# High-part passes of two weight tiles first, chunk inputs ahead of the taps on TensorE, third modulations ahead of the layer norm, and late small inputs

## The reference, cut to what matters

```python
def ada_mod(c, w, b):                      # modulations from the condition c
    return jax.nn.silu(c) @ w + b

def trunk_layer(x, c, conv_buf, h0_re, h0_im, lp):
    sh1, sc1, g1, sh2, sc2, g2 = jnp.split(ada_mod(c, w_ada, b_ada), 6, axis=-1)
    h = modulate(rms_norm(x, norm1_g), sh1, sc1)
    z = h @ w_in                           # 1024 -> 512 (a), 512 (gate), 512 (u)
    hc = a * jax.nn.sigmoid(gate)
    hc, new_buf = causal_depthwise_conv(hc, conv_buf, conv_w, conv_b)   # width 31
    hc = jax.nn.silu(layer_norm(hc, conv_ln_g, conv_ln_b))
    hs, hT_re, hT_im = s5_mixer(u, h0_re, h0_im, ...)   # 32 groups x 64 complex states
    mix = jnp.concatenate([hc, hs], axis=-1) @ w_out
    x = x + g1[:, None, :] * mix
    h2 = modulate(rms_norm(x, norm2_g), sh2, sc2)
    x = x + g2[:, None, :] * peer_ffn(h2, peer_w_q, peer_keys, peer_u, peer_v)
    return x, new_buf, hT_re, hT_im
```

## Time and profile before

| what | value |
|---|---|
| runs shown, median of 3 | 1868.39 us (1866.77 to 1869.2) |
| profiled execution, its own time | 1861.53 us |
| its span, first to last instruction | 1859.7 us |
| mean granted TensorE clock, share of full | 0.983 |
| TensorE matmuls busy | 1758.6 us (95%) |
| VectorE busy | 1186.8 us (64%) |
| ScalarE busy | 681.9 us (37%) |
| GpSimd busy | 689.5 us (37%) |

### The profile page before, as it was taken

How to read it: one execution, slowest core, us unless ns; L and a number is a source line. 1 busy time by engine, 2 the same in 40 slices (tenths; PEclk the granted TensorE clock), 3 DMA queues, 4 the chain that set the end, 5 groups by cost and what they waited for, 6 DMA issues and landing times.

```text
span 1859.7 us, 33440 instructions
## 1 busy us (share of the span) xinstructions
PE 1758.6 (95%) x13287; PEld 1635.7 (88%) x13287; DVE 1186.8 (64%) x3089; ACT 681.9 (37%) x1212; POOL 689.5 (37%) x585
## 2 busy tenths in 40 slices
PE   5997868999999999999999999999999999999996
PEld 2884557889999999999999999988888888888895
DVE  8987953159995677777776760256666666666663
ACT  2313323233333444444444444333333333333333
POOL 1200013335446333333333334466555555555200
PEclk9999889999999999999999999999999999999998
DMA  8454322548888788888888788689988889888831
GB/s 300 119 122 159 131 100 80 181 152 241 239 242 234 211 245 253 260 248 248 256 238 256 250 255 245 230 288 361 340 321 317 319 311 338 327 315 316 303 126 47
DMA packets 305707, 442.72 MB, mean 238 GB/s; under 512 B 24752, under 2 KB 221536, under 8 KB 303504
## 3 DMA queue, kind: packets, MB, share of 16 engines
q1 hardware_dynamic: 280416, 366.35, 61.8%
q0 software_dynamic: 25136, 74.24, 11.3%
HBM read 377.37 MB, written 130.25 MB: 273 GB/s over the span
## 4 chain that ended last, share of the span: by engine, by line
PE 88%; DVE 7%; DMA 2%; ACT 2%; issue 1%; POOL 1%; DVEq 0%; SPq 0%; ACTq 0%; POOLq 0%
PE ps L1823 40%; PE ps L1851 28%; PE ps L1582 8%; PE ps L1812 5%; PE ps L1802 3%; DVE conv_out L1146 1%; PE ps L1553 1%; PE ps L1536 1%; PE ps L1638 1%; DVE rstd L1052 1%; DMA v_rows_ring<-v_rows,v_row_index 1%; DMA raw<-in_w_ada 1%; PE ps L1722 0%; PE ps L1771 0%; DVE wt L928 0%
## 5 line engine op out<-in xcount | busy, mean ns | idle before, releaser
L1823 PE MATMUL ps<-h,hl 128*128 128x256 f32 (+1 forms) x6144 | 823.7, 288 | 1.4 <-DVE sc L1312 1.4
L1823 PEld LDWEIGHTS ps<-h,hl 128*128 128x128 f32 x6144 | 761.7, 189 | 1.6 <-DVE sc L1312 1.6
L819 ACT ACTIVATE hl<-raw 128x512 fp32r<-128x512 f32 x512 | 322.4, 630 | 730.3 <-PE ps L1823 475.6
L1851 PEld LDWEIGHTS ps<-WH,hl 128*128 128x128 f32 x3072 | 531.7, 188 | 30.3 <-issue 28.5
L1851 PE MATMUL ps<-WH,hl 128*128 128x384 f32 x3072 | 545.1, 337 | 1.3 <-ACT actr L851 1.3
L618 POOL TENSOR_TENSOR hl<-raw,hl 128x512 fp32r<-128x512 f32 x260 | 352.2, 1356 | 500.5 <-ACT hl L819 500.5
L1492 DVE TENSOR_TENSOR hl<-raw,hl 128x512 fp32r<-128x512 f32 x252 | 174.7, 693 | 231.9 <-ACT hl L819 231.7
L1421 DVE TENSOR_SCALAR ohA<-ps,selT 128x128 f32<-128x128 f32 x384 | 133.8, 349 | 146.3 <-PE ps L1812 133.6
L635 POOL DMA_INDIRECT v_rows_ring<-v_rows,v_row_index x136 | 130.0, 956 | 202.8 <-PE ps L1802 170.4
L626 POOL DMA_INDIRECT gathered_act<-act_spill,act_index x136 | 151.9, 1117 | 43.4 <-issue 41.3
L1422 DVE TENSOR_SCALAR ohB<-ps,selT 128x128 f32<-128x128 f32 x384 | 154.1, 401 | 0.0
(11 more groups left out here) (281 smaller groups left out, 1295.4 us busy)
## 6 DMA issues: line engine op xcount, KB each, us to landing
raw<-in_u SPq DMA_DIRECT2D x128, 512.0 KB, 6.7
v_rows<-in_v SPq DMA_DIRECT2D x128, 512.0 KB, 5.8
raw<-in_v SPq DMA_DIRECT2D x128, 512.0 KB, 5.9
act_spill<-actr SPq DMA_DIRECT2D x128, 260.0 KB, 2.8
raw<-in_w_ada SPq DMA_DIRECT2D x64, 512.0 KB, 4.4
gate_spill<-stage SPq DMA_DIRECT2D x24, 1024.0 KB, 7.6
hring<-act_spill SPq DMA_DIRECT2D x128, 192.0 KB, 3.8
gbp<-gate_spill SPq DMA_DIRECT2D x16, 1536.0 KB, 7.7
```

The costliest lines, as they stand in the source:

```text
L819: act.activation(hl[:, n % 2, 0, c], raw[:, n % NRAW, c], ACT.Copy).then_inc(s_whi, 1)
L1823: last = pe.matmul(ps[:, 2 * (m % 2) + h, 0:b - a], hl[:, m % 2, w, q * P:(q + 1) * P], h2[:, r, q, a:b], start=q == 0 and (w, r) == (0, 0 ...
L1851: last = pe.matmul(ps[:, mm % 2, 0:ND], hl[:, mm % 2, w, j * P:(j + 1) * P], WHL[b % 2][:, r, j, :], start=j == 0 and (w, r) == (0, 0), st ...
```

## The change

It has four parts and two small ones.

1. `split_dense`: for `in` and `q`, the passes with the high part of the rows (both weight parts) of tiles 0 and 1 are run first, waiting block by block for the rounded rows (`s_h`) only; then tile 0's pass with the low part, then tile 1's. VectorE makes all eight normed blocks first (in the input projection with the two weight splits after the second and the seventh) and all low parts behind them. ScalarE's two weight copies move to behind the first and the fifth shift.
2. The chunk inputs, with the first four tiles of modulation pair 1, move in front of step 12 of the loop `e`, and the tap matmuls behind them; ScalarE's copies move alike. Ten of VectorE's taps move from before S to behind it (`AFTER_SCAN` 24 instead of 18, the rest at the end), and taps alternate between the first and the last unfinished tile.
3. Modulation pair 2 is multiplied before the layer norm's sums (seven q) and between them (the eighth); none is left behind output tile 0. Each normed conv block is split one block behind its norm.
4. Modulation pair 3 is one q ahead in the query projection, in the stream too; ScalarE copies its rows before the last query tile and takes that tile's result before the first retrieval tile's high part.
5. The small inputs of the conv and the state (`cw`, `cvec`, `h0`, four of `stc`) are loaded behind the first four input tiles, under a semaphore of their own.

```diff
-AFTER_SCAN = 18
+AFTER_SCAN = 24
-          + tiles_of("q", 0, 1) + ada(3, 0, 1)
-          + [tile for f in range(2, KD) for tile in tiles_of("q", f) + ada(3, f - 1, f)]
-          + ada(3, KD - 1, KD))
+          + tiles_of("q", 0, 1) + ada(3, 0, 2)
+          + [tile for f in range(2, KD) for tile in tiles_of("q", f) + ada(3, f, f + 1)])
...
             for n in range(NRAW, NPRE):
+                if n == FIRST["in"] + NRAW:
+                    for name, t in (("cw", cw[:]), ("cvec", cvec[:]), ("h0", h0[:])):
+                        sp.dma_start(t, dr[name]).then_inc(s_late, 16)
+                    for c in range(CT):
+                        sp.dma_start(stc[:, c, :, 0:CW - 1], dr["stc"][:, c]).then_inc(s_late, 16)
...
-            split_hi(FSP["in"], hlm)
             for k in range(KD):
                 act.wait_ge(s_hs, k + 2)
                 act.activation(rhi[:, k, 0:TP], h1[:, k, 0:TP], ACT.Identity,
                                bias=mods[:, SH1 + k, 0:1]).then_inc(s_h, 1)
-                if k == 2:
+                if k == 0:
+                    split_hi(FSP["in"], hlm)
+                if k == 4:
                     split_hi(FSP["in"] + 1, hlm)
...
             for k in range(KD):
+                if k == KD - 1:
+                    modulation_rows(3)
                 act.wait_ge(s_q, k + 1)
                 if k + 2 < KD:
                     split_hi(FSP["q"] + k + 2, hl)
-                else:
-                    peer_hi(k + 2 - KD, 0)
-                    peer_hi(k + 2 - KD, 1)
...
                 last.then_inc(s_qe, 1)
-            modulation_rows(3)
+                if k + 2 >= KD:
+                    peer_hi(k + 2 - KD, 0)
+                    peer_hi(k + 2 - KD, 1)
...
-                    t = min(left[0:2], key=lambda u: taps[u])
+                    pair = (left[0], left[len(left) - 1])
+                    t = pair[1] if pair[0] == latest[0] else pair[0]
...
+            dve.wait_ge(s_late, 16 * NLATE)
             conv_rows(0)
...
-            conv_taps(6, tuple(range(CT)))
...
-            conv_taps(4, tuple(range(CT)))
             dve.wait_ge(s_Ve, 6)
...
+                if t:
+                    conv_split(t - 1)
+            conv_split(CT - 1)
...
                     if kind == "out" and t == 0:
-                        products(0, 0, 0, CT)
+                        products(0, 0, 0, CT, ORDER)
                         pe.wait_ge(s_lo, k + 2)
-                        products(1, 2, 0, CT)
-                    early = kind == "out" and t < 2
-                    products(t, bank, CT if early else 0, KD).then_inc(sem_, 1)
+                        products(1, 2, 0, CT, ORDER)
+                    if kind != "out" and t == 0:
+                        pe.wait_ge(s_h1s if kind == "in" else s_h2s, 1)
+                        products(0, bank, 0, KD, HIGH, (s_h, 1 if kind == "in" else KD + 1))
+                        pe.wait_ge(s_lo, k + 2)
+                        products(1, in_bank(1) if kind == "in" else 2, 0, KD, HIGH)
+                    if kind != "out" and t < 2:
+                        last = products(t, bank, 0, KD, LOW, None if t else (s_h1l if kind == "in" else s_h2l, 2))
+                    else:
+                        early = kind == "out" and t < 2
+                        last = products(t, bank, CT if early else 0, KD, ORDER)
+                    last.then_inc(sem_, 1)
                     then(t)
+            HIGH, LOW = ((0, 0), (1, 0)), ((0, 1),)
+            ORDER = HIGH + LOW
...
             split_dense("in", hlm, (rhi, h1lo), None, s_win)
-            modulation_rows(1, 0, 2)
...
+            def chunk_inputs():
+                pe.wait_ge(s_prepe, 12)
+                pe.wait_ge(s_hc, CT)
+                pe.wait_ge(s_ul, 16 * (L + 2))
+                for t in range(ST):
+                    for g in range(2):
+                        for a in range(2):
+                            c = (t % 6) * (NC + 2 * TS)
+                            last = pe.matmul(ps[64 * g:64 * g + 64, 3 * a + t // 6, c:c + NC + 2 * TS],
+                                             ET[:, a, t, 64 * g:64 * g + 64], U[:, 2 * t + g, :], start=True, stop=True)
+                last.then_inc(s_V, 1)
...
             for e in range(20):
-                if e == 4:
+                if e == 12:
+                    chunk_inputs()
+                    modulation_rows(1, 0, 2)
+                    pe.wait_ge(s_Ve, 6)
                     conv_partial_sums()
...
-            modulation_rows(2, 0, 5)
+            modulation_rows(2, 0, KD - 1)
...
-            modulation_rows(2, 5, 6)
+            modulation_rows(2, KD - 1, KD)
...
-                if t == 0:
-                    modulation_rows(2, 6, KD)
                 if t == 4:
                     modulation_columns(2)
...
-            split_dense("q", hl, (h2[:, 0], h2[:, 1]), s_qe, s_q, lambda t: modulation_rows(3, t, t + 1))
+            split_dense("q", hl, (h2[:, 0], h2[:, 1]), s_qe, s_q, lambda t: modulation_rows(3, t + 1 if t else 0, min(t + 2, KD)))
```

More of the change, by code:

```diff
@@ L76 @@
 HR = 2
-NSMALL = 11
+NSMALL = 4
+NLATE = 7
 NMOD = 64
@@ L724, in _ @@
             for e in range(20):
-                if e == 4:
+                if e == 12:
+                    act.wait_ge(s_V, 1)
+                    for a in range(2):
+                        for b in range(3):
+                            t0, t1 = 6 * b, min(6 * b + 6, ST)
+                            act.activation(V[:, a, t0:t1, :].rearrange("p t c -> p (t c)"),
+                                           ps[:, 3 * a + b, 0:(t1 - t0) * (NC + 2 * TS)], ACT.Copy).then_inc(s_Ve, 1)
                     act.wait_ge(s_cp, 1)
@@ L1130, in _ @@
             tapped_at = [0] * CT
+            latest = [CP]
             def conv_taps(count, tiles):
@@ L1289, in h2_low @@
                                          h2[:, 0, q, 0:TP].bitcast(F32), ALU.add, ALU.subtract).then_inc(s_h2l, 1)
-            def h2_lows(q):
-                if q == 0:
-                    dve.wait_ge(s_h2s, 1)
-                    dve.tensor_tensor(h2[:, 1, :, TP:T], h2f[:, :, TP:T], h2[:, 0, :, TP:T].bitcast(F32),
-                                      ALU.subtract).then_inc(s_h2l, 1)
-                else:
-                    h2_low(q - 1)
-            apply_norm("rms2", h2f, SH2, h2_lows)
-            h2_low(KD - 1)
+            apply_norm("rms2", h2f, SH2)
+            dve.wait_ge(s_h2s, 1)
+            dve.tensor_tensor(h2[:, 1, :, TP:T], h2f[:, :, TP:T], h2[:, 0, :, TP:T].bitcast(F32), ALU.subtract)\
+                .then_inc(s_h2l, 1)
+            for q in range(KD):
+                h2_low(q)
             modulations(3)
@@ L1570, in split_dense, with products @@
                     bank = in_bank(t) if kind == "in" else 2 * (t % 2)
-                    def products(tile, bank, first, last_):
+                    def products(tile, bank, first, last_, passes, ready=None):
                         for i in range(first, last_):
@@ L1576, in products @@
                                 pe.wait_ge(s_rl, max(1, i - CT + 2))
-                            if kind != "out" and tile == 0:
-                                pe.wait_ge(s_h1l if kind == "in" else s_h2l, i + 2)
-                            for w, r in PASSES:
+                            if ready is not None:
+                                pe.wait_ge(ready[0], ready[1] + i)
+                            for w, r in passes:
                                 for h, (a, b) in enumerate(HALVES):
@@ L1677, in _ @@
             pe.wait_ge(s_prepe, 20)
-            pe.wait_ge(s_ul, 16 * (L + 2))
-            for t in range(ST):
-                for g in range(2):
-                    for a in range(2):
-                        c = (t % 6) * (NC + 2 * TS)
-                        last = pe.matmul(ps[64 * g:64 * g + 64, 3 * a + t // 6, c:c + NC + 2 * TS],
-                                         ET[:, a, t, 64 * g:64 * g + 64], U[:, 2 * t + g, :], start=True, stop=True)
-            last.then_inc(s_V, 1)
             modulation_rows(1, 3, 5)
```

45 lines of the change are left out of this document (19 added, 26 removed).

## The result

| | before | after |
|---|---|---|
| median of the runs, us | 1867.58 (1866.55 to 1869.2, 4 runs) | 1851.65 (1850.77 to 1854.43, 4 runs) |
| ratio of the times | | 0.9915 (95% interval 0.9899 to 0.993) |
| profiled execution, us | 1861.53 | 1852.28 |
| its span, us | 1859.7 | 1850.4 |

The two profiled executions differ by only 9.3 us (9.25 in time, 9.3 in span). That the two gains are not the same is the finding to explain, and the experiments begin there.

What follows compares the result with a forecast made beforehand. Retrieval keeps TensorE busy from about 396 us, so TensorE's waits before it set the gain. 5.5 + 1.2 + 5.1 + 0.8 - 0.5 = 12.1 us off 1868.39 gives 1856.3, range 1853 to 1864.

Steps and rivals of the forecast that it cites:

- Late small inputs: First loads: moving seven small loads behind the fourth input tile neither wins nor costs time, 0 us.
- High passes in the input projection: Input projection: high-part matmuls first need only the shifts, 1.3 us won (0 to 2.7), ending at 121.5.
- The gap goes: S5 preparation, tap matmuls: TensorE's 5.28 us idle time without a releaser, taken as a late instruction packet, falls to 0.
- S 7.1 earlier: S5 preparation: with chunk inputs ahead of the taps, the states S come at 181.4, 7.1 us earlier.
- Conv sums 5.5 + 1.2: Sums over conv rows: 5.5 us won (4 to 6.5) at their start, 1.2 more as the last two run faster.
- TensorE's sums of the conv rows released by a modulation load: Sums over conv rows: a sign listed as showing the forecast wrong; no size given.
- Third output tile 5.1 + 0.8: Output tiles: third starts at 266.3 in place of 271.43, 5.1 us won, and itself takes 0.8 less.
- Query projection -0.5: Query projection: 2.2 us lost at query tile 2's load, 1.2 to 1.7 won at the end; range -2 to +2.5.
- The gap stays: Tap matmuls: rival, the 5.28 us gap remains, S only 1.8 earlier, gain 6.8, time 1861.6 us; chance 0.19.
- more gaps: Chunk inputs and taps: rival, several 5.28 us gaps; from the third on slower, 1872.1 us; chance 0.06.
- The output tile stays late: Output tiles: rival, S no earlier and GpSimd late too, 1 to 3 us left, 1866.5 us; chance 0.09.
- Query tile 2 in time: Query projection: rival, that tile's load lands sooner, 2.5 us more won, 1853.8 us; chance 0.06.

Runs made afterwards that it cites:

- a_stores: Changed kernel with GpSimd's five small stores of the conv states started only once the chunk states S are ready: 1850.61 us, ratio 0.9892 to the kernel before.
- b_stores: Kernel before with GpSimd's five small stores of the conv states started only once the chunk states S are ready: 1859.77 us, ratio 0.9951.
- a_gap: Changed kernel with the five conv state stores held until the chunk inputs are through TensorE, so beside the taps again: 1856.58 us, ratio 0.9938 to the kernel before.
- the last three runs: Changed kernel with VectorE's second modulations behind S and 12 taps (1844.35 us), then also third modulation tiles spread (a_S_ln), then nine taps more ahead (a_S_ln_t).
- a_S_ln: Changed kernel with VectorE's second modulations behind S and the third modulation tiles spread around the conv sums: 1844.64 us, ratio 0.9878 to the kernel before.
- a_S_ln_t: a_S_ln with nine more conv taps ahead of VectorE's first weight split (33 instead of 24): 1837.74 us, ratio 0.9841 to the kernel before.
- b_again: Kernel before, unchanged, timed and profiled a second time: ratio 0.9997, span of the profiled execution 1864.0 us.
- b_look2: Kernel before, unchanged, profiled a third time: 1865.61 us, span 1863.8.
- only3: Kernel before with only the third modulation tiles ahead of the layer norm and the conv splits interleaved with the norm's products: 1861.55 us, ratio 0.9966.

## Why the prediction was wrong

**The step that failed** is the last line of the sum: "The median of the runs shown, 1868.39, is 6.9 higher; less 12.1 it is 1856.3." It took the 6.9 us as a constant of the measurement that the change leaves alone. After the change the profiled execution lies 0.6 us above its median. Of the 6.9 some 4 were time in the part that was changed, or in chance around it: two more profiles of the kernel before are 4.3 us slower at the first retrieval matmul than the one I read. One of them lost 2.5 us more in and behind the gap, the other 2.1 us more in the sums by the clock; both lost 1.4 to 1.8 in the first loads. Against these two the changed kernel gains 13.6 us by its profile, against the one I read 9.35. The changed kernel's profile has chance in it as well: quick first loads (its projection ends 1.3 us before the mean of the seven with the high passes first) and slow sums of the conv rows (5.46 us, 3.77 in a_stores), which nearly cancel. What is left up to the 15.9 of the medians, 2.3 us, was not traced: these two executions, 1865.79 and 1865.61 us, still lie below most timed runs of their kernel, whose medians here are 1867.6 to 1869.8.

The terms, one by one, by the profile:

- *Late small inputs, 0: not to be told apart.* The transposes of the first modulations start at 41.6 to 45.4 in the eight profiles with this part and at 42.4 to 44.7 in the six without. The reason given was wrong in one point: TensorE's first waits are for modulation loads (up to 2.54 us between 31 and 42 us before the change, 2.85 after), not for VectorE.
- *High passes in the input projection, 1.3: right.* The projection ends at 121.65 instead of 122.84. The end itself scatters by more than that from profile to profile, with the first loads; from the transposes of the first modulations to the end it is 80.4 to 81.4 us in the seven profiles without the high passes first and 79.4 to 79.9 in the seven with, 1.2 less by the means.
- *The gap goes: right, and its cause with it,* by b_stores and a_gap. Its size was short: my chain took it at 8.27 + 5.28 + 1.98 - 9.2 = 6.3 us. It costs 6.8 to 9.5, since TensorE's clock stands at 0.50 behind it, and 9 us by the medians. The rule of the Trainium skill that I set against it (Runtime: NRT & Kernel Launch, Instruction fetch mechanics: the crossing of a block of instructions is mostly hidden) did not hold in the taps: 4.5 to 7.2 us beside these small stores, and 0.4 to 1.5 without them in the changed order; in b_stores it did. Had it decided, the forecast would have been further off, 1861.6.
- *S 7.1 earlier: 4.9.* The chain was the right one (VectorE's modulations behind TensorE's transposes), but S came 2.2 later than worked out. The four modulation tiles at 1.9 us took 1.8. It was the last six, behind the first direct products, that waited for loads: 8.2 us (164.91 to 173.09) instead of the 6.8 that they took before, within a stretch of 13.4 that I carried over as it was. The other 0.8 had gathered ahead of the direct products.
- *Conv sums 5.5 + 1.2: 1.8.* This is the term of the sum that failed. I had named its risk (four tiles at 1.2 to 1.7 us) with the first two sums ending at 229.2 to 231.2 and the last two 2.0 later; all four ended at 237.7. Before, the first sum stood at 229.47; 4.9 earlier is 224.6; it came at 232.27, so the four tiles took 1.9 us each, and after that wait the four sums took 5.46 us, not 4.0, at a granted clock of 0.54 in their first half. Of the 4.9 us missing some 2.2 came with S, 1.2 from the pace of the four tiles and 1.5 from the clock. The listed sign, "TensorE's sums of the conv rows released by a modulation load", is what the profile shows; but the taps, late with S, ended at 232.19 instead of 229.7, so by these rows the last sums would have waited for them without the loads too.
- *Third output tile 5.1 + 0.8: 5.0 + 1.3, right.* It starts 6.85 earlier, less the 1.8 that come from the sums, and takes 6.0 us (to 270.6) instead of 7.37. GpSimd's low part ends at 264.52, as TensorE comes to the tile, so no wait shows; in a_stores it waited 0.88 us, for GpSimd.
- *Query projection -0.5: +1.1 in this profile.* TensorE stops at 304.03 + 3.09 = 307.1 and starts the scores at 376.03, 68.9 us later; before it was 385.38 - 323.47 + 8.11 = 70.0. Of it 0.8 is the earlier start (7.32 us of waiting instead of 8.11), and at the end 1.31 of waiting for ScalarE went. The 2.2 forecast as lost are there, but before a modulation tile that stands behind query tile 2 in the stream (2.17), and not before tile 2. Over the six profiles with this part whole it is 68.9 to 70.5 us, over the six with the old projection 70.0 to 70.3, so that +0.4 is the better figure.

So the terms come to 9.35 by these two profiles where 12.1 were forecast. By them alone the answer would have been 1859, within the range; that it lay below is due to the base, which had 6.6 us more in it that went with the change, 4.3 of them seen in the other two profiles. That the forecast missed by no more than 4.6 is luck in part, since the two errors have opposite signs.

**The rivals.** "The gap stays" was wrong, "more gaps" too. "The output tile stays late" was wrong as well. "Query tile 2 in time" came true for the tile, but not for the time: the wait fell on a modulation tile instead. That the conv sums would be paced by loads I had only as a bound of my forecast and not as a rival with a price.

**What bounds the kernel after the change** the last three runs show: two streams that meet at the conv sums, taps on VectorE and modulation tiles on TensorE. Spreading the tiles alone brings nothing (a_S_ln); with nine taps more ahead as well it is 7 us (a_S_ln_t). The taps alone were not run. Before both stood an order: S behind modulations that it does not need, 17.58 us of VectorE and 5.83 of TensorE.

## What to carry to other kernels

Before a predicted saving is taken off a median, ask why the profiled execution differs from it: a profile that lies below every timed run has left out something that varies, and if the change touches that, the offset can go with it. A second profile of the kernel before would have shown 4 of the 6.9 us. A gap without a releaser is tested cheaply by moving what fills the DMA engines in front of it; here one wait on GpSimd gave 9 us. When a reordering leaves an engine idle (VectorE, 17.58 us), look at what stands first behind the idle time and whether the work that others wait for needs it.

## What was not expected of the hardware

- Small stores that fill the DMA engines (share around 1 at 38 to 105 GB/s) stop TensorE where it runs some 40 records of small matmuls a microsecond: 4.5 to 7.2 us in five profiles (first profile, b_again, b_look2, only3, a_gap), never in those where the stores ran elsewhere (at most 1.5). The packet of the instruction queue starts 9.1 to 10.9 us behind the one before it in the four of these with the order of before, and 3.6 in b_stores.
- Behind such a gap, and behind waits of 2 us around the layer norm, the granted clock is 0.50 (1.2 GHz; 0.52 and 0.54 as means of stretches of 3 us) for some microseconds in one execution and 1.00 (2.4 GHz) in another. The same sixteen records take 3.89 or 5.46 us, the scores 9.18 or 10.75: 1.57 us each time, and an order that costs TensorE a short wait can cost that much more. The Trainium skill (TensorE: Matmul & The Clock Gate, The HAM clock gate) says of a kernel's start that its slow matmuls vary from run to run; these traces show the same in the middle of one.
- The loads of the first modulations differ from execution to execution so that the input projection ends up to 3 us earlier or later, more than most of the parts of this change are worth.
